# Two blocks on one core: the first block's mixers trade buffers, and its projections are reordered

## The reference

```python
proj = h @ w_in
aq, ak, av, bq, bf, bv, bg, cqkv, cg, cb, ca = jnp.split(proj, split_at, axis=-1)
aq = partial_rope(rmsnorm(aq, q_norm), positions)        # 8 heads; ak: 2 heads
out_a = sliding_window_attention(aq, ak, av, sinks)
log_f = jnp.logaddexp(jnp.log(lb), jnp.log1p(-lb) + jax.nn.log_sigmoid(bf))
out_b = rmsnorm(hgrn2_chunked(bq, log_f, bv), hgrn_norm) * jax.nn.silu(bg)
cqkv = jax.nn.silu(causal_depthwise_conv(cqkv, conv_w))  # then l2norm of q and k
beta, g = sigmoid(cb), -exp(a_log) * softplus(ca + dt_bias)
out_c = rmsnorm(gated_delta_chunked(cq, ck, cv, beta, g), gdn_norm) * jax.nn.silu(cg)
y = jnp.concatenate([out_a, out_b, out_c], axis=-1) @ w_out
```

## Time and profile before

| | us |
|---|---|
| median of 3 runs | 4292.32 |
| lowest, highest | 4284.3, 4299.93 |
| span of the profiled execution | 4287.7 |
| mixers of layer 0, in the profile | 521.2 |
| mixers of layer 1, in the profile | 518.5 |

### The profile page before, as it was taken

How to read it: one execution, slowest core, us unless ns; L and a number is a source line. 1 busy time by engine, 2 the same in 40 slices (tenths; PEclk the granted TensorE clock), 3 DMA queues, 4 the chain that set the end, 5 groups by cost and what they waited for, 6 DMA issues and landing times.

```text
span 4287.7 us, 51835 instructions
## 1 busy us (share of the span) xinstructions
PE 3992.2 (93%) x20700; PEld 3250.2 (76%) x20700; DVE 2571.8 (60%) x4066; ACT 1621.0 (38%) x2881; POOL 108.0 (3%) x199
## 2 busy tenths in 40 slices
PE   5879999998889999999999999999899999999988
PEld 5759778877768788887777677767777777777776
DVE  6767365654576432456667743776566667546765
ACT  3343232243443332333444243553334343334532
POOL 0000000000000000000000000000000000000000
PEclk9979799998899799989999999999899999999999
DMA  6502155532111232333232223233232322221233
GB/s 219 171 5 89 50 168 196 188 118 65 60 40 69 72 101 84 106 100 104 91 99 72 74 89 94 64 104 126 80 119 85 108 70 84 84 88 56 84 113 113
DMA packets 216641, 417.93 MB, mean 97 GB/s; under 512 B 16384, under 2 KB 61472, under 8 KB 214608
## 3 DMA queue, kind: packets, MB, share of 16 engines
q1 hardware_dynamic: 197584, 335.12, 24.4%
q0 software_dynamic: 18816, 79.49, 5.4%
HBM read 378.89 MB, written 35.67 MB: 97 GB/s over the span
## 4 chain that ended last, share of the span: by engine, by line
PE 80%; DVE 12%; ACT 5%; issue 2%; DMA 1%; SPq 0%; DVEq 0%; ACTq 0%; POOLq 0%
PE ps L632 59%; PE ps L104 13%; DVE arena L126 3%; PE ps L115 3%; ACT arena L200 3%; DVE arena L141 2%; DVE spl L126 2%; PE ps L2292 2%; DVE X L126 1%; DVE HF L126 1%; DVE sm L147 1%; PE ps L2287 1%; ACT sph L200 1%; PE ps L882 1%; PE ps L110 1%
## 5 line engine op out<-in xcount | busy, mean ns | idle before, releaser
L126 DVE TENSOR_TENSOR spl<-ring,sph 128x1024 fp32r<-128x1024 f32 (+2 forms) x556 | 651.5, 1178 | 731.9 <-ACT sph L200 730.7
L200 ACT ACTIVATE sph<-ring 128x1024 fp32r<-128x1024 f32 (+2 forms) x556 | 562.4, 1023 | 776.6 <-PE ps L632 758.3
L632 PE MATMUL ps<-sph,HTh 128*128 128x512 f32 (+3 forms) x1680 | 668.9, 398 | 22.6 <-DVE HTl L126 11.7
L632 PE MATMUL ps<-spl,HTh 128*128 128x512 f32 (+3 forms) x1680 | 621.5, 370 | 0.0
L632 PE MATMUL ps<-sph,HTl 128*128 128x512 f32 (+3 forms) x1680 | 620.6, 369 | 0.0
L200 ACT ACTIVATE arena<-ps 128x512 f32<-128x512 f32 (+2 forms) x570 | 314.0, 563 | 727.8 <-PE ps L632 484.3
L632 PE MATMUL ps<-HTh,sph 128*128 128x512 f32 x1360 | 540.5, 397 | 17.1 <-DVE spl L126 14.9
L632 PE MATMUL ps<-HTl,sph 128*128 128x512 f32 x1360 | 532.5, 392 | 0.0
L632 PE MATMUL ps<-HTh,spl 128*128 128x512 f32 x1360 | 532.1, 391 | 0.0
L104 PE MATMUL ps<-arena 128*128 128x128 f32 (+6 forms) x2264 | 374.0, 349 | 52.3 <-ACT arena L200 29.9
L632 PE MATMUL ps<-sph 128*128 128x512 f32 x992 | 405.6, 409 | 7.4 <-DVE spl L126 7.4
(11 more groups left out here) (219 smaller groups left out, 5105.3 us busy)
## 6 DMA issues: line engine op xcount, KB each, us to landing
ring<-in_w_in SPq DMA_DIRECT2D x264, 512.0 KB, 3.6
arena<-in_ada_w SPq DMA_DIRECT2D x88, 512.0 KB, 4.7
ring<-in_w_down SPq DMA_DIRECT2D x44, 512.0 KB, 3.3
ring<-in_w_gate SPq DMA_DIRECT2D x40, 512.0 KB, 3.8
ring<-in_w_up SPq DMA_DIRECT2D x40, 512.0 KB, 3.8
ring<-in_w_mem SPq DMA_DIRECT2D x32, 512.0 KB, 3.3
ring<-in_w_out SPq DMA_DIRECT2D x32, 512.0 KB, 3.9
ring<-in_w_br_ssd SPq DMA_DIRECT2D x32, 512.0 KB, 3.9
```

The costliest lines, as they stand in the source:

```text
L126: self.e.tensor_tensor(o, a, b, op).then_inc(*self.done.up())
L200: self.e.activation(o, a, f, **kw).then_inc(*self.done.up())
L632: ins = pe.e.matmul(o, l, r, start=k0 == 0 and i == 0 and not b.pairs, stop=k0 + b.ks == b.kt and i == 3 * b.ks - 1 and (c0 > 0 or not b.p ...
```

## The change

The blocks of the main stream stand in another order: `hzb`, `c`, `cgb`, `hvb`, then `q` and `kvb`. The delta rule's `TOK` and `G5` move to the arena's start, attention's `QKT`, `AV`, `PT` and small buffers and the delta rule's `AT` and `QT_` go to `HF`, and the memory tokens lie over the recurrence's space; so `mem` follows `hgrn`, and the main stream stops before the output projection for `att`. The recurrence's and the delta rule's first steps are parted by more yields. `att` may start after `kvb`, which is now last.

```diff
-        QK, QKT, AV, PT = ar(0, 4, 640), ar(2560, 5, 512), ar(5120, 4, 128), ar(5632, 4, 512)
+        QK, QKT, AV, PT = ar(5120, 4, 640), hf(2560, 5, 512), hf(7168, 4, 128), hf(5120, 4, 512)
...
                 a.cp(QK[:, m, 512:640], p[:, 0:128], par=True)
+                a.wait_ge(at[("kvb", l), 3])
                 at["kv", l] = a.cp(AV[:, m, :], p[:, 128:256], par=True)
...
-            KVs = ar(O_ATT, 2048)
+            KVs = ar(O_HG + 6144, 2048)
...
-        MT_ = ar(O_ATT, 8, 256)
-        MTS = tuple(ar(O_ATT + 2048 + 2048 * i, 8, 256, of=ARr) for i in range(2))
+        MT_ = ar(O_HG, 8, 256)
+        MTS = tuple(ar(O_HG + 2048 + 2048 * i, 8, 256, of=ARr) for i in range(2))
...
-            p.wait_ge(at["pv", l, 7], at["kv", l])
+            p.wait_ge(at["hfin_t", l, 3])
...
             a.act(E_, CUM, ACT.Exp, scale=-1.0)
-            a.act(LU, E_, ACT.Ln, bias=1.0)
-            at["softplus", l] = a.act(W_, LU, ACT.Exp, scale=-1.0)
             if l:
                 e0, e1 = sm[:, 532:534], sm[:, 534:536]
                 a.wait_ge(at["lbs", l])
                 a.act(e0, e0, ACT.Exp)
                 at["lbe", l] = a.act(e1, e1, ACT.Exp)
+            a.act(LU, E_, ACT.Ln, bias=1.0)
+            at["softplus", l] = a.act(W_, LU, ACT.Exp, scale=-1.0)
+            yield
+            yield
+            if l:
...
         def hgrn_pe(pe, l):
-            yield (5 if l == 0 else 9, 5 if l == 0 else 7)
-            yield (3.5, 0)
+            yield (0, 6.5)
+            yield (4 if l == 0 else 9, 0)
+            yield (0, 0 if l == 0 else 2.4)
+            yield (3.5 if l == 0 else 5, 0)
...
-        TOK, G5, AT = hf(0, 4, 768), hf(3072, 4, 512), hf(5120, 4, 512)
+        TOK, G5, AT = ar(0, 4, 768), ar(3072, 4, 512), hf(0, 4, 512)
...
-            yield (2, 2.8)
+            yield (0.5, 1.6)
+            yield (0, 4.2)
+            yield (0.6, 0)
...
-            a.wait_ge(at[("hvb", l, 1), 3])
...
-            starts = [("conv", (), {0: conv[1], **conv}), ("gdn", ("conv",), slot_after(name, ("hvb", l, 1))),
+            starts = [("conv", (), {0: conv[1], **conv}),
+                      ("gdn", ("conv",), {6: slot_after(name, ("cgb", l, 2)), 17: slot_after(name, ("kvb", l))}),
                       ("att", (), slot_after(name, ("kvb", l))),
-                      ("hgrn", (), {0: slot_after(name, ("hzb", l, 1)), 8: ("att", 99), 22: slot_after(name, ("hvb", l, 1))}),
-                      ("inv", ("gdn",), 0), ("mem", ("att",), 0),
-                      ("back", ("inv",), 0)]
+                      ("hgrn", (), {0: slot_after(name, ("hzb", l, 1)), 22: slot_after(name, ("hvb", l, 1))}),
+                      ("inv", ("gdn",), 0), ("mem", ("hgrn",), 0),
+                      ("back", ("inv",), slot_after(name, ("mv", l, 3)))]
...
-            return {slot_after(k, ("hvb", l, 1)): [("mem", 99)], w: [("hgrn", 99)], w + 8: [("inv", 99)]}
+            return {slot_after(k, ("kvb", l)): [("mem", 99)], w: [("att", 99)], w + 8: [("inv", 99)]}
```

More of the change, by code:

```diff
@@ L1025, in mix_blocks @@
                      for i in range(2)]
+            w_in += [Block(("q", l, j), W, 256 * j, 256, 8, HT, dict(dve=q_dve(j)), ready=HTR, **by4) for j in range(2)]
+            w_in.append(Block(("kvb", l), W, 512, 256, 8, HT, dict(act=kv_act), ready=HTR, **by4))
             MEM, W = [("memhi", l), ("memlo", l)], T["w_mem"][l]
@@ L1091, in att_dve @@
             yield
-            rt = [ar(6912 + 80 * i, 80).rearrange("p (h d) -> p h d", d=8) for i in range(4)]
+            rt = [HFf[:, 7720 + 80 * i:7800 + 80 * i].rearrange("p (h d) -> p h d", d=8) for i in range(4)]
             for m in range(4):
@@ L1292, in hgrn_dve @@
             c1 = c1s[:, l, :]
+            if l:
+                l0, l1 = c1[:, C1["lb0"]:C1["lb0"] + 2], c1[:, C1["lb1"]:C1["lb1"] + 2]
+                mx, e0, e1, sm2, lb, om = [sm[:, 530 + 2 * i:532 + 2 * i] for i in range(6)]
+                v.tt(mx, l0, l1, ALU.max)
+                v.tt(e0, l0, mx, ALU.subtract)
+                at["lbs", l] = v.tt(e1, l1, mx, ALU.subtract)
+            yield
             v.wait_ge(at["softplus", l])
@@ L2023, in first @@
                 ht_begin(q, k, xn, [(k, "xn", m) for m in (0, 1, 2, "half", 3)])
-            weave(q, k, main(q, k), mixers(q, l), mix_gates(l), CHAIN, slot_after(k, ("hvb", l, 1)))
+            weave(q, k, main(q, k), mixers(q, l), mix_gates(l), CHAIN, slot_after(k, ("kvb", l)))
             k = ("ffn", l)
```

46 lines of the change are left out of this document (23 added, 23 removed).

## The result

The changed kernel takes 4345.67 us (median of 4 runs, 4340.92 to 4351.75) against 4292.74 before: a ratio of 1.0125, 95% interval 1.0111 to 1.0139, 53 us slower. The forecast was 4298 within 4268 to 4332; the chance for slower was 0.35. The profiled execution has a span of 4349.9 us against 4287.7, 62.2 more. It is the slowest of its four runs, and that of before was faster than its median, so differences of rows come out some 9 us larger than the difference of the medians.

What follows compares the result with a forecast made beforehand. TensorE, busy 93% of the span, was taken as the bound. Layer 0 at +7 and layer 1 at -1 gave +6 us on the profiled 4287.7, so 4294, and 4298 as median against 4292.3; range 4268 to 4332.

Steps and rivals of the forecast that it cites:

- the part behind: Memory projections to the end of the output projection: as long as TensorE's work, 192 us in layer 0, 206 in layer 1.
- The second stretch alone: Side work alone between memory and output projections, 38.3 and 44.0 us before: to be gone in both layers.
- the rival of the faster clock: Delta rule's state steps among memory tiles run at full clock, 24 us a layer saved, 4250; chance 0.07.
- X: X's return from DRAM before its first use in the output projection: a possible stall, cost 0, bound 5 us.
- The projections of layer 1: TensorE's 12.85 us gap before the convolution weights shrinks to 6 to 8: 6 us off, bounds 0 and 13.
- The projections of layer 0: No such gap before; convolution, recurrence's start and angles meet in the first 60 us: 0, bounds -4 and +6.
- The first stretch alone: Side work alone before the memory projections, with the recurrence from its third level: 163 and 146 us, 41 and 31 more.
- the 175 and 158: Sign of a wrong forecast: side work alone before the memory projections over 175 us in layer 0, 158 in layer 1.
- first part: Side work alone up to the recurrence's chunk products: VectorE's work plus 9 and 11 us idle, 101 and 100 us.
- second part: Side work alone from the recurrence's chunk products on: as long as TensorE's work, 62 and 46 us.
- the rival of the round trips: ScalarE's round trips leave VectorE idle 21% up to the recurrence's chunk products: +28 us, 4326; chance 0.28.
- the forecast case: All terms as forecast, 4298, the same as before; with the terms' bounds 4286 to 4305; chance 0.43.

Runs made afterwards that it cites:

- split_only: The kernel before with only the recurrence's parted first steps, in both layers; 4282.8 us, ratio 0.9976.
- diag_late: The changed kernel with layer 0's first recurrence chunk products planned 14 us of VectorE work behind the step before, instead of 3.5; 4323.5 us, ratio 1.0080.
- two_chains: The changed kernel with the recurrence held after its tenth step until attention is over; 4350.0 us, ratio 1.0142.
- pred_half: The changed kernel with VectorE's 28 masked copies a layer in the recurrence's level steps half as wide (output not the reference's); 4331.2 us, ratio 1.0096.
- fill: The changed kernel with eight useless 128-column matmuls on TensorE before each of the recurrence's 14 level products; 4353.0 us, ratio 1.0137.
- tables: The changed kernel with four kinds of ScalarE functions replaced by absolute values, 39 table loads instead of 59; 4333.8 us, ratio 1.0094.

## Why the prediction was wrong

**What bounds the kernel, and the part behind.** Right. Memory to the end of the output took 188.4 and 204.5 us against 192 and 206; there TensorE's work is the time. The second stretch alone is gone in layer 0 and down to 8.5 us in layer 1. The state steps ran at a low clock again, so the rival of the faster clock had nothing for it. X came back in time: no such wait shows.

**The projections of layer 1.** Right in kind: the gap before the convolution weights fell to 3.58 us instead of the 6 to 8 forecast, and the stretch by 10.3 us instead of 6. split_only shows that the parting alone does it.

**The projections of layer 0, forecast at 0 within -4 and +6.** Wrong: +9.8. I had written that the convolution, the recurrence's start and the angles meet in the first 60 us, and priced that at nothing. The parted step also moved TensorE's diagonal products ahead of projection tiles, by `yield (3.5 ...)`, to a place where VectorE had some 9 us of other work ahead of taking up their first half, and so of freeing the banks for the second. I had asked who waits for the parted functions, not what TensorE has in its queue behind them: 8.48 us at 117.32. diag_late took all but 1.5 us of the wait away, and with it and the waits behind it 14 us of the projections.

**The first stretch alone.** This is the step that failed: 193.7 and 170.1 us against 163 and 146, 54.8 us where the whole miss is 56. Both lie beyond the 175 and 158 that I had named as signs of being wrong, and VectorE was busy 0.72 and 0.70 of it instead of 0.86. Of the 54.8 us, 18 are the first part's (25 of VectorE's idle time, less 7 of its work that I had too high in layer 1), and 36 the second part's, which I took for as long as TensorE's work, with chunk steps of 3.5 us as in the earlier trace rows.

- Its first part was forecast at 101 and 100 us, VectorE's work of 92 and 89 us with 9 and 11 idle. VectorE's work was 92.7 and 81.7 us. Its idle time was 23.0 and 22.0, 20 and 21% of the part. That is the share which I had given to the rival of the round trips and had read from the earlier trace rows; I preferred 11% because I held that a third chain fills the holes of the other two. two_chains contradicts it: with two at a time the mixers are as long. pred_half shows that the load counts besides. Even that rival, 4326, fell short, since it left the second part as forecast.
- ScalarE's round trips, which I had named for that rival, are what VectorE waited for: by the waits, 23.7 of 26.2 us in layer 1's first part end with a result of ScalarE, and 17.3 of 23.7 in layer 0's. (A wait is put down to the result that came last; ScalarE waited for VectorE's results in its turn.) Its table loads are a small part of that: some 13 us for 20 loads, of which my forecast had counted some already. The longest waits in layer 1's first part (total, times, longest) are attention's first root (part of it ahead of the stretch), the gates, sums (L147) behind a function of ScalarE and the tail of the recurrence:

```profile
DVE HF L147 <- ACT HF L200: 9.4, 1, 9.4
DVE sm L135 <- ACT sm L200: 4.5, 1, 4.5
DVE sm L147 <- ACT arena L200: 4.2, 2, 2.3
DVE arena L126 <- ACT arena L200: 3.3, 1, 3.3
```

- Its second part was forecast as long as TensorE's work, 62 and 46 us, and took 78.0 and 66.4. Taking each step at the mean time that its form had in before, TensorE's work in it comes to some 63 to 66 and 53 to 55 us, an estimate: 1 to 4 us more than I had in layer 0, 7 to 9 in layer 1. The low clock then added some 5 to 8 and 8 to 9 us (0.82 and 0.74), and 6.9 and 4.1 us were idle. Layer 1's share of that clock differs from one profile to the next (58.4 us at 0.86 in two other runs). I had costed the chunk steps at full clock, "about 3.5", from a row in which the clock was high, though the earlier trace rows showed 0.81 over the stretch in which they then stood. The sum had a term for the clock that goes with the second stretch alone (-5.7 in layer 1) and none for where the same narrow matmuls go.

**The sum.** Of the 56 us between the forecast's +6 and the profiled +62, by the stretches: projections 9.8 - 4.3, first parts 14.7 and 3.7, second parts 16.0 and 20.4, the rest -3.6 and -1.5, together 55. The other terms' misses cancel, which is luck; the four of the two stretches all lie on one side, since each took the order as better covered, or the clock as higher, than it was. The range ended at 4332 since its slowest case was the idle share alone, at +28, with no case in which it came together with layer 0's projections (bound +6) and the clock. The span given for the forecast case, 4286 to 4305, was too narrow too: with +6 in either projection and 5 for X its own terms reach 4315.

What remains open: how much of the first part's idle time is the fixed order and how much the latency of each hand-off; no run here separates them. Nor does fill separate the clock's part in it from the filler's own time.

## What to carry to other kernels

A stretch in which VectorE is busy 79% with two chains was not filled by a third one here: price it with the idle share that the trace shows for the chains that meet there (73 to 74% for attention with the delta rule, 98 to 99% for the recurrence with the inverse), and take a better share only if a row shows those chains at work together. A parted step must be followed on every engine: the part that helped ScalarE and VectorE in layer 1 put TensorE's products in layer 0 where their banks came free late. And when steps move, their clock moves with them: cost narrow matmuls by the clock of the stretch that they stood in and by that of the stretch they go to, not by the best row.

## What the runs showed of the hardware

A low clock with a TensorE that is not idle: in the delta rule's state steps of the changed kernel, most of them matmuls of 64 columns, with one memory tile among them, it was busy 19.83 of 20.00 us at a clock of 0.50, half speed.

```profile
530.00:550.00 20.00, 19.83 (x81) 17.18 (x81) 4.67 (x12) 5.07 (x11) 0.00 (x0) 0.50 0.02 2
```

The same matmuls in the same order found another clock in other profiles: layer 1's second part ran at 0.74 in 66.40 us in the changed kernel, at 0.78 in 63.80 us in diag_late, whose edit leaves layer 1 alone, and at 0.86 in 58.40 us in tables and pred_half, whose TensorE order is the same there. diag_late's row:

```profile
1255.50:1319.30 63.80, 60.67 (x309) 46.26 (x310) 38.24 (x79) 30.50 (x70) 0.53 (x1) 0.78 0.05 17
```

What made the difference is not shown, since each kernel has one profile. It is up to 8 us, 0.2% of the kernel, and a stretch of one profile can't be compared with another's to better than that.
